# Head norms: the squares are summed in 32x32 blocks by VectorE, and TensorE adds four quarters with a product of 16 columns

## The reference

```python
def rmsnorm(x, g):
    xf = x.astype(jnp.float32)
    y = xf * lax.rsqrt(jnp.mean(xf * xf, axis=-1, keepdims=True) + EPS)
    return (y * g.astype(jnp.float32)).astype(x.dtype)

    h = rmsnorm(x, g_mix) @ w_in
    z, xbc, dt, q, k, v, qi, ki, wi = _split(h, IN_SIZES)
    ...
    q = rmsnorm(q.reshape(b, l, ATT_HEADS, ATT_HEAD_DIM), g_q)
    k = rmsnorm(k.reshape(b, l, ATT_KV_HEADS, ATT_HEAD_DIM), g_k)
    v = v.reshape(b, l, ATT_KV_HEADS, ATT_HEAD_DIM)
    qi = qi.reshape(b, l, IDX_HEADS, IDX_HEAD_DIM)
    ki = rmsnorm(ki, g_kidx)
    ...
    y_att = dsa_attention(q, k, v, qi, ki, wi)
```

## Time and profile before

| | us |
|---|---|
| median of 3 runs | 2645.39 (2644.92 to 2645.55) |
| the profiled execution | 2646.74 |
| its span, from first to last instruction | 2644.9 |
| TensorE busy in the span | 2619.3 (99%) |
| VectorE busy | 1850.1 (70%) |
| ScalarE busy | 1308.5 (49%) |
| GpSimd busy | 207.9 (8%) |
| one product L673 (two passes), to the next product's start | 0.86 |
| stage with the six products L673 | 82 to 154 us of the span |

### The profile page before, as it was taken

One profiled execution on the slowest core, in us unless ns is written; L12 is line 12 of the kernel. 1 busy time (PEld: TensorE's weight loads), 2 busy tenths in 40 slices (PEclk: granted clock), 3 DMA queues, 4 the chain that ended last, 5 costly groups with the idle time before them and its releaser, 6 DMA issues. The chain is left out here.

```text
span 2644.9 us, 33873 instructions
## 1 busy us (share of the span) xinstructions
PE 2619.3 (99%) x13464; PEld 2224.6 (84%) x13464; DVE 1850.1 (70%) x2669; ACT 1308.5 (49%) x1807; POOL 207.9 (8%) x182
## 2 busy tenths in 40 slices
PE   9999999999999999999999999999999999999998
PEld 8788888888888888888889888988888888888887
DVE  7788797846748567786776767566668567486585
ACT  6545455535445344465555445455555344453453
POOL 4014001000000000140411300000000000000000
PEclk9999999999999999999999999999999999999999
DMA  7644445555555555566334333355555555555553
GB/s 268 164 179 161 162 168 183 199 191 191 197 187 189 207 191 192 185 249 253 143 123 150 114 128 128 128 213 183 191 200 191 197 187 197 191 191 197 187 205 127
DMA packets 68165, 481.78 MB, mean 182 GB/s; under 512 B 8007, under 2 KB 8135, under 8 KB 11176
## 3 DMA queue, kind: packets, MB, share of 16 engines
q1 hardware_dynamic: 65520, 467.43, 49.3%
q0 software_dynamic: 1968, 10.75, 1.5%
q10 hardware_dynamic: 520, 1.43, 0.1%
HBM read 473.29 MB, written 6.29 MB: 181 GB/s over the span
## 5 line engine op out<-in xcount | busy, mean ns | idle before, releaser
L1299 DVE TENSOR_TENSOR w_lo<-weight_ring,w_hi 128x1024 fp32r<-128x1024 f32 x882 | 1084.9, 1241 | 613.3 <-ACT w_hi L2155 609.8
L2155 ACT CAST w_hi<-weight_ring 128x1024 fp32r<-128x1024 f32 x884 | 917.9, 1049 | 721.6 <-PE bank L553 580.9
L541 PE MATMUL bank<-mix,w_hi 128*128 128x512 f32 x1776 | 568.7, 402 | 2.2 <-DVE arena L1371 1.0
L551 PE MATMUL bank<-w_hi,h 128*128 128x512 f32 x1056 | 412.5, 391 | 0.0
L551 PE MATMUL bank<-w_hi,mix 128*128 128x512 f32 x1056 | 411.2, 389 | 0.0
L553 PE MATMUL bank<-w_hi,h 128*128 128x512 f32 x1056 | 411.0, 389 | 0.0
L552 PE MATMUL bank<-w_lo,h 128*128 128x512 f32 x1056 | 410.9, 389 | 0.0
L552 PE MATMUL bank<-w_lo,mix 128*128 128x512 f32 x1056 | 410.9, 389 | 0.0
L553 PE MATMUL bank<-w_hi,mix 128*128 128x512 f32 x1056 | 410.8, 389 | 0.0
L544 PEld LDWEIGHTS bank<-mix,w_lo 128*128 128x128 f32 x1776 | 334.3, 188 | 78.9
L544 PE MATMUL bank<-mix,w_lo 128*128 128x256 f32 x1776 | 350.2, 279 | 0.0
(11 more groups left out here) (376 smaller groups left out, 2012.5 us busy)
## 6 DMA issues: line engine op xcount, KB each, us to landing
weight_ring<-in_w_up SPq DMA_DIRECT2D x128, 1024.0 KB, 4.8
weight_ring<-in_w_down SPq DMA_DIRECT2D x128, 1024.0 KB, 4.7
weight_ring<-in_w_merge SPq DMA_DIRECT2D x32, 1024.0 KB, 4.8
weight_ring<-in_w_gdn SPq DMA_DIRECT2D x24, 1024.0 KB, 4.8
weight_ring<-in_w_papb SPq DMA_DIRECT2D x16, 1024.0 KB, 4.8
weight_ring<-in_w_o SPq DMA_DIRECT2D x16, 1024.0 KB, 4.8
weight_ring<-in_w_xbc SPq DMA_DIRECT2D x12, 1024.0 KB, 4.8
weight_ring<-in_w_q SPq DMA_DIRECT2D x8, 1024.0 KB, 4.8
```

The costliest lines, as they stand in the source:

```text
L541: e.matmul(bank[:, :], w_hi[:, unit_at % UNITS, o + j * P:o + (j + 1) * P], x[:, :, at + j * S:at + (j + 1) * S], start=first and j == 0, ...
L551: e.matmul(out, x[:, 0, at:at + m], hi, start=first, stop=False)
L1299: e.tensor_tensor(w_lo[:, i, :], ring[:, p % PIECES, half * UNIT:(half + 1) * UNIT], w_hi[:, i, :].bitcast(F32), ALU.subtract).then_inc(un ...
L2155: e.copy(w_hi[:, i, :], ring[:, p % PIECES, half * UNIT:(half + 1) * UNIT]).then_inc(unit_hi, 1)
```

## The change

The sum over 128 partitions is done in two stages. VectorE turns the squares themselves in 32 x 32 blocks (L1447 of the new code, from SBUF instead of from PSUM) and adds each block's row of 32 with a new TENSOR_REDUCE (L1449), which gives 128 x 16 partial sums: each partition holds a sum over one quarter of the channels. TensorE's product (L676) has then 16 columns instead of 512; its stationary operand `quarters` adds the four quarters. ScalarE's root reads the 16 columns from PSUM, and the reciprocal works on a small buffer (`head_inverse`). Two instructions ahead of the loop make `quarters` from the identity matrix.

```diff
             def head_sums():   # TensorE
                 for s in range(1, 7):
                     yield from rounds(4)
-                    e.wait_ge(head_squared, s + 1)
-                    if s > 1:
-                        e.wait_ge(head_turned, s - 1)
-                    e.matmul(psum[6][:, :], ones[:, :], sq_1[s % 2], start=True, stop=True).then_inc(head_summed, 1)
+                    if s == 1:
+                        e.wait_ge(quarters_made, 2)
+                    e.wait_ge(head_parted, s)
+                    e.wait_ge(head_root, s)
+                    e.matmul(psum[6][:, 0:16], quarters, head_parts, start=True, stop=True).then_inc(head_summed, 1)
...
             def head_norms():   # VectorE
+                e.wait_ge(params_loaded, 48)
+                e.tensor_reduce(quarter, mat("ident").rearrange("p (q w) -> p w q", w=32), AX_X,
+                                ALU.add).then_inc(quarters_made, 1)
+                e.wait_ge(quarters_made, 1)
+                e.tensor_copy(split(quarters, 4), over(quarter, 4)).then_inc(quarters_made, 1)
...
                 for s in range(1, 7):
                     yield from rounds(3)
-                    e.wait_ge(head_summed, s + 1)
-                    e.transpose(head_turn, psum[6][:, :]).then_inc(head_turned, 1)
+                    e.wait_ge(head_squared, s + 1)
+                    e.transpose(head_turn, sq_1[s % 2]).then_inc(head_turned, 1)
+                    e.wait_ge(head_turned, s)
+                    e.tensor_reduce(head_parts, head_turn.rearrange("p (b w) -> p b w", w=32), AX_X,
+                                    ALU.add).then_inc(head_parted, 1)
                     yield
...
-                    e.reciprocal(block_rows(head_turn), block_rows(head_turn)).then_inc(head_inv, 1)
+                    e.reciprocal(head_inverse, head_inverse).then_inc(head_inv, 1)
                     e.wait_ge(head_inv, s + 1)
-                    e.transpose(root_1, block_rows(head_turn).to_broadcast([P, 16, 32])).then_inc(head_spread, 1)
+                    e.transpose(root_1, wide(head_inverse, 32)).then_inc(head_spread, 1)
...
             def head_norms():   # ScalarE
-                    if s >= 2:
-                        e.wait_ge(head_summed, s - 1)
+                    if s > 2:
+                        e.wait_ge(head_turned, s - 2)
                     e.activation(sq_1[s % 2], pair(arena[:, X_AT:], s - 1), ACT.Square).then_inc(head_squared, 1)
                     yield from rounds(2)
-                    e.wait_ge(head_turned, s)
-                    e.activation(block_rows(head_turn), block_rows(head_turn), ACT.Sqrt, bias=eps[:, 0:1],
+                    e.wait_ge(head_summed, s + 1)
+                    if s > 1:
+                        e.wait_ge(head_spread, s - 1)
+                    e.activation(head_inverse, psum[6][:, 0:16], ACT.Sqrt, bias=eps[:, 0:1],
                                  scale=1.0 / P).then_inc(head_root, 1)
```

More of the change, by code:

```diff
@@ L339, in build @@
          st1), at = places(kept_1, QI_T * S, 2 * S, 512, 512, 512, 512, P, S, P, S, 8, 512, 512, 32, 512, 512, 8, 8)
-        head_turn = conv_acc_1
+        head_turn, head_parts, head_inverse = conv_acc_1, pt0[:, 0:16], pt0[:, 16:32]
         score, sel_neg, relu_buf, sq_1 = [score0, score1], [sel0, sel1], [relu0, relu1], [sq0, sq1]
+        (quarters, quarter), at = places(at, P, 32)
         hot_at = X_AT - (XBC_T + Z_T) * S - 2 * S - NSA_HEADS
@@ L477, in build @@
         head_root, head_inv, ki_rooted = sem("head_root"), sem("head_inverse"), sem("ki_rooted")
-        head_turned, head_spread = sem("head_sums_turned"), sem("head_inverse_spread")
+        head_turned, head_parted = sem("head_squares_turned"), sem("head_squares_summed_in_quarters")
+        head_spread, quarters_made = sem("head_inverse_spread"), sem("quarters_made")
         rows_summed, rows_copied, rows_written = sem("bias_rows_summed"), sem("bias_rows_copied"), sem("bias_rows_written")
@@ L734, in attention @@
                         e.wait_ge(dec_dve, DEC["dve"]["last"])
-                        e.wait_ge(head_turned, 6)
+                        e.wait_ge(head_root, 7)
                     else:
```

## The result

| | before | after |
|---|---|---|
| median, us | 2645.59 (2644.92 to 2647.81, 8 runs) | 2653.69 (2651.18 to 2654.44, 8 runs) |
| the profiled execution | 2646.74 | 2654.32 |
| its span | 2644.9 | 2652.5 |

The changed kernel is slower: ratio 1.0026, 95% interval 1.0017 to 1.0036, which is 4.5 to 9.5 us with its middle at 6.9; the medians lie 8.1 us apart. The forecast was 2651.0 in a range up to 2653.6, so the direction was right and the size 2.7 us short, a hair beyond the range.

The account below looks back on a forecast made before the run. TensorE was taken to bound the kernel, busy 2619.3 of 2644.9 us. Products -3.84, place 1 +4.85, clock +1.7 and place 6 +2.9 gave +5.6 on 2645.4: 2651.0 us, range 2647.8 to 2653.6.

Parts of the forecast that it names:

- making of `quarters`: Two VectorE setup instructions between two `w_lo`, ahead of the first head-norm product, were to make it 0.55 us later.
- place 1, product later by: First of the six head-norm products: it would start at 87.7 instead of 82.88 us, +4.85 us.
- wait there: At the first head-norm product TensorE would stand idle for 5.7 us until VectorE's sum is ready.
- first fall of the clock: Behind the wait at the first head-norm product, TensorE's clock would fall to half, costing 1.7 us.
- six short products: The six head-norm products, 16 columns instead of 512, would each save 0.64 us of TensorE, -3.84 us in all.
- place 6, wait: At the last head-norm product, behind VectorE's top-k selection, TensorE would wait 3.0 us against 0.15 before, +2.9 us.
- rival 2: The clock falls a second time, behind the last head-norm product: 1.7 us more, 2652.7 us; chance 0.25.
- given back in attention: Attention, behind the head norms, is driven by TensorE, so its later waits would move along and give nothing back.
- Places 2 to 5: The second to fifth head-norm products would have no wait for the sum, the third being the tightest.
- Rival 1: Waits at the first and last head-norm products but no fall of the clock: +4.0 us, 2649.4 us; chance 0.15.
- Rival 3: Later waits in attention and the SSD shrink and give back 2.6 us: +3.0 us, 2648.4 us; chance 0.12.
- Rival 4: VectorE is early enough at every head-norm product, only the savings remain: -3.8 us, 2641.6 us; chance 0.03, still less time included.

Follow-up runs that it names:

- e3: The changed kernel with the two VectorE instructions that make `quarters` moved to the end of the third round: 2653.14 us, ratio 1.0023.
- e2: The changed kernel with VectorE's turn and sum moved to the end of the round before, TensorE's program unchanged: 2646.85 us, ratio 1.0005.
- e4: The changed kernel with products nobody reads ahead of the waiting product, 12 at place 1 and 6 at place 6: 2650.26 us, ratio 1.0016.
- e10: The changed kernel with products nobody reads ahead of the waiting product, 24 at place 1 and 11 at place 6: 2649.84 us, ratio 1.0014.
- e8: The kernel before with products at places 2 to 6 cut to 16 of 512 columns, the other sums left out: 2642.59 us, ratio 0.9990.
- e12: Quarters only at places 2 to 4, product one round later; old product at 1, 5, 6; `quarters` made behind the third round: 2643.98 us, ratio 0.9993.
- e1: The changed kernel with product, root and scaling two rounds later at places 1 and 6, one round later at 2 to 5: 2646.42 us, ratio 1.0001.
- e6: The changed kernel with VectorE's reduction done twice at places 2 to 4, the extra result unread: 2652.88 us, ratio 1.0025.
- e5: The changed kernel with the old 512-column product and the turn behind it at places 1 and 6: 2646.22 us, ratio 1.0004.

## Why the prediction was right in direction and short in size

**Step by step.** All of after, counted from `ki`'s product:

| term | predicted | measured |
|---|---|---|
| making of `quarters` (within place 1) | 0.55 | 0.58 (e3) |
| place 1, product later by | +4.85 | +4.89 |
| wait there | 5.7 | 5.57 |
| first fall of the clock | +1.7 | +1.94 |
| six short products | -3.84 | -3.64 |
| place 6, wait (less 0.15 before) | +2.9 | +2.3 |
| second fall, behind place 6 | rival 2, +1.7 | +1.15 |
| given back in attention | 0 | 0 |

The measured terms add to 6.6 us, the stage's 6.65, but that is no check of them: the term of the second fall is what the stretch from place 6 to attention has left over against before (18.3 against 17.8 us, with 0.6 us for the shorter product). Measured against kernels with the short product and no fall there (e2, e4 and e10, 16.7 us), the second fall costs 1.6 us; the difference is time that before, e8 and e12 (17.7 to 17.8 us) lose in this stretch, which I put down to VectorE's pace without a run that shows it. The first fall, from place 1 to place 2 against e10, is 2.0 us. Place 1 went as told: the new product waits for a turn that stands behind `w_lo`. e1 and e2 confirm it by moving the one or the other. TENSOR_REDUCE took 0.69 us for 16 columns as for 2, and the turn 0.71 us from SBUF. Lines and shapes of DVE after (busy us, mean ns, idle before; answers to the earlier trace rows):

```profile
L1447 DVE STREAM_TRANSPOSE arena<-arena 128x512 f32<-128x512 f32 x6 | 4.2, 706 | 0.0
L1449 DVE TENSOR_REDUCE arena<-arena 128x16 f32<-128x512 f32 x6 | 4.1, 686 | 0.2
```

Places 2 to 5 had no wait, as said, with place 3 not alone in being tight: the sums were there 1.9, 1.2, 1.3 and 0.2 us ahead of the products, so place 5 was the closest. I had called its pattern the same as that of place 3 without working it out. For place 6 the chain over the lift, the addition and the selection gave a product 6.3 us later measured from place 6 of before; it came 6.1 us later counted from `ki`.

**The step that failed is the price of the clock.** The sum has one fall behind place 1 and no more; a second one was rival 2, with 0.25. It came, behind 2.5 us of idleness, in the profile of after and in those of e3 and e6. e10 gives both together: 3.7 us against the 1.7 in the forecast. The wait of place 6 takes 0.6 us of that back: 2.3 us against 2.9. Of the rows I had, idle times of 2.31 and 1.7 us were followed by a fall, and the argument I set against rival 2, that TensorE is fully busy on both sides of place 6, had no row behind it. The clock fell all the same. By those rows two falls were the likelier case, 2652.7 us.

**The rest, about 1.6 us, is not explained.** The stage gives 6.65 us of the 8.1 between the medians, and 0.2 us is the median of before, 2645.6 here and 2645.4 in the forecast. The profiled executions lie 7.6 us apart, 0.3 us of it ahead of the stage and 0.6 behind. What can move a run by more is the fall near 1187 us: after, with it, has a run of 2654.3 us; e6, with nearly the same stage and without it, 2651.5. The eight runs of after lie at 2651.2 to 2651.4 (three) and at 2653.4 to 2654.4 (five); those of before at 2644.9 to 2646.3 (six) and at 2647.3 and 2647.8. That this fall sorts them is a guess, and by the mean granted clock of the runs it is not the whole of it. That clock is 0.998 in the three lower runs of after and 0.996 in the five others, a difference of at least 0.001, while a fall that costs 1.7 us changes the mean over 2652 us by 0.0006. So something else of the clock differs between these runs too, and they have no trace. The fall near 1187 us was there in 5 of 13 profiled executions, with stages from 103.0 to 109.7 us; whether a shift of 6 us makes it more frequent stays open.

**Rival 1 (no fall of the clock) is refuted** by the windows. e10 gives its price: with the waits in place and no fall the stage is 2.9 us longer than before, where the rival had 4.0; its product of place 6, counted from `ki`'s, comes 4.0 us later than before, where the rival had 4.6.

**Rival 3 (given back) is refuted** by the table of rests: 2473.0 us in e6, 2472.7 to 2473.2 in every other kernel without the late fall. A stage 8 us longer gives nothing back in attention. The wait at L762 is 2.6 us in after, as before.

**Rival 4 (savings only) was right to get little chance, for a reason that I had not seen.** I had priced it at -3.8 us, as if each shorter product were worth its full length once VectorE is early. e1 made VectorE early and its stage was 0.2 us shorter than before; e8, without any new work on VectorE, 1.9 us. TensorE is 99% busy over the span, but in this stage the three engines share one pace: VectorE's stretch from place 5 on in the kernel before (length, busy us and count, then as above) has 27.4 us of work in 28.5, the rest being the steps from one instruction to the next:

```profile
142.00:170.50 28.50, 27.40 (x72) 1.00 0.45 161
```

What is taken from TensorE meets that. The share of busy time over the span does not tell it; the stretch at the end of the stage does.

## What to carry to other kernels

When a sum is moved from a product to VectorE ahead of the product, ask where in VectorE's own order the new step stands, and what each instruction queued ahead of it waits for: here a turn behind one `w_lo` made a 0.2 us product wait 5.6 us, while twice the work at an idle moment cost nothing. An engine at 99% of the span gains from a shorter instruction only as far as the next engine is ahead of it at the end of that stage, and that is read from the gaps of the other engines there. A wait of more than 2 us on TensorE can cost a second time, through the clock behind it (here 1.6 to 2.0 us each time), so put that into the sum or say which row speaks against it. Compare kernels from a point where their runs still agree.

## What the hardware showed

**The clock of TensorE.** Idle time of TensorE, and the granted clock in the 4 us stretch behind it, in this study:

| idle, us | where | granted clock behind it |
|---|---|---|
| 5.57 | after, place 1 | 0.50 |
| 3.62 | e2, place 1 | 0.68 |
| 2.83 | e4, place 1 | 0.63 |
| 2.49 | after, place 6 | 0.60 |
| 2.24 | after, first product behind the start | 0.82 and, in the next 4 us, 0.75 |
| 3.51 | e8, the same place | 1.00 and 1.00 |
| 1.7 | before and after, L965 | 0.57 and 0.62 |
| 1.7 | e6, L965 | 1.00 |
| 1.79 | e5, place 3 | 1.00 |
| 1.66, 1.61 | e1 | 1.00 |
| 1.14 | e4, place 6 | 1.00 |

Values between 0.5 and 1 are stretches in which the clock was at 1.2 GHz for a part and at 2.4 GHz for the rest. In the stage it fell at every idle time of 2.49 us and more, in all kernels that have one. At 1.6 to 1.8 us it fell only at L965, and there not in every execution. But idle time alone does not decide: at the start of the kernel TensorE is idle for 2.1 to 3.6 us in each of the thirteen profiled executions, and the clock fell in twelve of them. In e8 it stayed at 1.00 from the start up to the last product, behind 3.51 us of idleness:

```profile
9.56 0.50 PE L535 MATMUL bank<-mix,w_hi 128*128 128x512 f32 x1 [3.51 <-DVE mix L1380]
```

What makes the difference is not shown. The Trainium skill (TensorE: Matmul & The Clock Gate, section What's actually happening) says that the throttled state is the default and that activity releases it; the stage agrees, and e10, which keeps the array busy with products that nobody reads, keeps 1.00 throughout the stage.

**Small fp32 products.** The one with 16 columns takes 0.14 us to the next product's start in a stream (104.89 to 105.03 in after), 0.24 us where the next product is a weight product (159.38 to 159.62), and in spacing from place to place it was worth 0.62 us against 512 columns, not the 0.72 that 0.86 - 0.14 would give. The Trainium skill (TensorE: Matmul & The Clock Gate, section Back-to-back issue gap) gives 25 ns as the floor of one; two passes with a weight load each take 0.14 us here. What makes up this time is not shown. A product `ones` with `ones` of 128 columns takes 0.23 us in a row of its like (e4).

**The form of the operand did not matter on VectorE.** The turn of 128 x 512 takes 0.71 us from PSUM and 0.71 us from SBUF (L1447), and a reduction to 16 columns takes as long as one to 2.
